# Second attention of a two-block network: values stationary, turned weights moving, softmax weights divided before they are turned

## The reference, cut to what matters

```python
def mla_attention(h, w_a, q_a_gain, kv_a_gain, w_qb, w_kvb, q_gain, k_gain, w_out, pos):
    ...
    scale = MLA_QK_DIM ** -0.5

    def block(blk, qb):
        sc = jnp.einsum('bqhd,bkhd->bhqk', qb, k).astype(jnp.float32) * scale
        p = causal_softmax(sc, blk, s)
        return jnp.einsum('bhqk,bkhd->bqhd', p.astype(v.dtype), v)

    o = query_block_map(block, q)
    return o.reshape(b, s, MLA_HEADS * MLA_V) @ w_out
```

## Time and profile before

| | |
|---|---|
| median of three executions | 1521.01 us |
| the executions | 1524.47, 1521.01, 1520.43 us |
| span of the profiled execution | 1517.0 us (its own time is not among those listed) |
| TensorE busy | 1321.8 us, 87% |
| VectorE busy | 664.2 us, 44% |
| ScalarE busy | 275.4 us, 18% |
| mean granted TensorE clock | 0.948 of 2.4 GHz |
| DMA | 512.58 MB, mean 338 GB/s |
| second attention, first turned weights to first `product` matmul | 666.89 to 701.51 us of the span |

### The profile page before, as it was taken

How to read it: one execution, slowest core, us unless ns; L and a number is a source line. 1 busy time by engine, 2 the same in 40 slices (tenths; PEclk the granted TensorE clock), 3 DMA queues, 4 the chain that set the end, 5 groups by cost and what they waited for, 6 DMA issues and landing times.

```text
span 1517.0 us, 25770 instructions
## 1 busy us (share of the span) xinstructions
PE 1321.8 (87%) x9790; PEld 825.2 (54%) x9790; DVE 664.2 (44%) x1596; ACT 275.4 (18%) x760; POOL 130.5 (9%) x199
## 2 busy tenths in 40 slices
PE   9999999767766779999999766767779999999997
PEld 4455565434433444566555433433344886899943
DVE  3874543211221222772543221221132634699976
ACT  2154111100100011362111100010011134222200
POOL 1312000000000000211000000000000133222100
PEclk9999999897988899999999988998899999999999
DMA  8978799999999999859799999999999980654400
GB/s 289 397 293 332 282 422 410 421 421 422 422 422 422 422 422 392 322 211 421 302 420 412 421 421 422 422 422 422 422 422 398 373 298 29 209 167 167 167 28 28
DMA packets 120379, 512.58 MB, mean 338 GB/s; under 512 B 12256, under 2 KB 46748, under 8 KB 69096
## 3 DMA queue, kind: packets, MB, share of 16 engines
q1 hardware_dynamic: 118576, 507.30, 83.9%
q0 software_dynamic: 1552, 4.06, 0.8%
q10 hardware_dynamic: 168, 0.09, 0.0%
HBM read 510.35 MB, written 1.07 MB: 337 GB/s over the span
## 4 chain that ended last, share of the span: by engine, by line
PE 36%; DMA 9%; SPq 8%; DVE 2%; issue 1%; POOL 0%; ACT 0%; POOLq 0%; DVEq 0%; ACTq 0%
DMA ring<-in_moe_w_up 9%; PE bank L2602 8%; SPq L1798 6%; PE bank L1365 5%; PE bank L2637 4%; PE bank L2219 3%; PE bank L439 2%; PE bank L451 2%; PE bank L1380 2%; PE bank L1351 2%; PE bank L1394 1%; SPq L1807 1%; PE bank L390 1%; PE bank L696 1%; PE bank L719 1%
## 5 line engine op out<-in xcount | busy, mean ns | idle before, releaser
L1365 PE MATMUL bank<-ring,hT 128*32 128x256 f32 (+1 forms) x2848 | 278.5, 456 | 137.9 <-DMA ring<-in_moe_w_up 74.3
L1365 PEld LDWEIGHTS bank<-ring,hT 128*32 128x32 f32 (+1 forms) x2848 | 146.8, 132 | 242.9 <-issue 183.4
L1645 DVE TENSOR_SCALAR pT<-pT 128x256 f32<-128x256 f32 x34 | 10.0, 294 | 441.8 <-ACT pT L1765 441.8
L1365 PE MATMUL bank<-BC,hT 128*32 128x256 f32 (+1 forms) x1120 | 141.3, 414 | 38.0 <-DMA ring<-in_moe_w_up 22.2
L1351 PEld LDWEIGHTS bank<-gtab,hn 128*128 128x128 f32 x1088 | 129.4, 192 | 15.4 <-issue 14.3
L1351 PE MATMUL bank<-gtab,hn 128*128 128x128 f32 x1088 | 132.6, 275 | 0.1
L1394 PE MATMUL bank<-hT,A 128*128 128x512 f32 x256 | 118.4, 605 | 0.0
L1380 PE MATMUL bank<-ring,gtab 128*32 128x512 f32 (+1 forms) x768 | 116.4, 595 | 0.9 <-ACT gtab L1759 0.9
L1365 PEld LDWEIGHTS bank<-BC,hT 128*32 128x32 f32 (+1 forms) x1120 | 73.1, 121 | 72.7 <-issue 54.0
L1765 ACT ACTIVATE pT<-bank 128x256 f32<-128x256 f32 x34 | 13.1, 384 | 484.4 <-PE bank L1365 484.4
L549 PE MATMUL bank<-ring,hT 128*128 128x512 f32 (+3 forms) x288 | 99.4, 505 | 0.3 <-DVE hT L313 0.2
(11 more groups left out here) (381 smaller groups left out, 1941.1 us busy)
## 6 DMA issues: line engine op xcount, KB each, us to landing
ring<-in_moe_w_gate SPq DMA_DIRECT2D x90, 1024.0 KB, 24.7
ring<-in_moe_w_up SPq DMA_DIRECT2D x88, 1024.0 KB, 25.5
ring<-in_moe_w_down SPq DMA_DIRECT2D x88, 1024.0 KB, 26.2
BC<-in_moe_w_gate SPq DMA_DIRECT2D x38, 1024.0 KB, 24.5
BC<-in_moe_w_up SPq DMA_DIRECT2D x32, 1024.0 KB, 25.0
BC<-in_moe_w_down SPq DMA_DIRECT2D x28, 1024.0 KB, 26.6
ring<-in_w_ada SPq DMA_DIRECT2D x24, 1024.0 KB, 14.8
ring<-in_w_up SPq DMA_DIRECT2D x22, 1024.0 KB, 5.8
```

The costliest lines, as they stand in the source:

```text
L1365: i = nc.tensor.matmul(GATE[q * cap:(q + 1) * cap, part * FF:(part + 1) * FF], xg[:, c, q * cap:(q + 1) * cap], u[:, c, :], start=(c == 0) ...
```

## The change

`o2` is made with `by_channel=True`. In the second attention:

- `weigh(i)` multiplies the item's weights in `SC` by `rden` right behind the reciprocal, on VectorE, and signals `mixed`; `turn(i)` waits for `mixed` and no longer for `exped`.
- `sum_v(i)` swaps its operands: the values are stationary, the turned weights move. The sum has channels on the partitions.
- `store(i)` is a plain copy to `hn`, by channel.
- `turn_heads` and `evac_heads` are left out for `o2`; `pieces` and `product` read `hn` head by head, each waiting for its own head's store. The 16 pieces stand two to an iteration from iteration 8 to 15.

```diff
+                self.by_channel, turns = by_channel, 0 if by_channel else TT
...
+            def channel(self, tt, c):
+
+                return hn[:, tt, c * P:(c + 1) * P] if self.by_channel else hT[:, c, tt * P:(tt + 1) * P]
...
             def heads_in(self, pe, tt, c):
+                if self.by_channel:
+                    self.heads_ready(pe, tt, c)
+                    return
...
             def tensor(self, pe, i, heads_ready):
 
+                if self.by_channel:
+                    self.heads_ready = heads_ready
+                    if i >= HEADS:
+                        self.pieces(pe, 2 * (i - HEADS), 2 * (i - HEADS) + 2)
+                    return
...
                 def turn(i):
                     tt, h, w = place(i)
-                    pe.wait_ge(*(mixed if mix else exped)(i + 1))
+                    pe.wait_ge(*(mixed if mix or by_channel else exped)(i + 1))
...
+                    if by_channel:
+                        for j in range(tt + 1):
+                            for m in range(outs):
+                                x = nc.tensor.matmul(out_bank[m * dv_w:(m + 1) * dv_w, 0:P], heads[h][1](j, m),
+                                                     turned_p[:, i % 3, m * w + j * P:m * w + (j + 1) * P],
+                                                     start=(j == 0), stop=(j == tt))
+                        x.then_inc(summed.sem, 1)
+                        return
...
             def heads_out(eng, tt, g):
-                if heads_ready:
+                if by_channel:
+                    eng.wait_ge(*stored(HEADS * tt + g + 1))
+                elif heads_ready:
...
-                    if i >= 3:
+                    if i >= 3 and not by_channel:
                         dve.wait_ge(*stored(i - 2))
                     dv.done(nc.vector.reciprocal(rden[:, i % 3, 0:maps], den[:, i % 3, 0:maps]))
+                    if by_channel:
+                        for m in range(maps):
+                            x = nc.vector.tensor_scalar(SC[:, i % 3, m, 0:w], SC[:, i % 3, m, 0:w],
+                                                        rden[:, i % 3, m:m + 1], None, ALU.mult)
+                        x.then_inc(mixed.sem, 1)
...
-                    if outs == 1:
+                    if by_channel:
+                        x = nc.vector.tensor_copy(dst, out_bank[:, 0:P])
+                    elif outs == 1:
...
-        o2 = OutStage(square_units(t["mla_w_out"][0], D, order="(c p)"), add_x)
+        o2 = OutStage(square_units(t["mla_w_out"][0], D, order="(c p)"), add_x, by_channel=True)
```

More of the change, by code:

```diff
@@ L392, in build, with __init__ @@
         class OutStage:
-            def __init__(self, blocks, add_to, heads_norm=None, gain=None):
+            def __init__(self, blocks, add_to, heads_norm=None, gain=None, by_channel=False):
                 self.blocks, self.add_to, self.heads_norm, self.gain = blocks, add_to, heads_norm, gain
+                self.by_channel, turns = by_channel, 0 if by_channel else TT
                 self.summed, self.added = shared("block_summed", 2), shared("block_added", 2 * TT)
-                self.turned = shared("turn_done", 4)
-                self.out_v, self.out_a = shared("turn_out_v", TT), shared("turn_out_a", TT)
+                self.turned = shared("turn_done", 2 * turns)
+                self.out_v, self.out_a = shared("turn_out_v", turns), shared("turn_out_a", turns)
+            def channel(self, tt, c):
+                return hn[:, tt, c * P:(c + 1) * P] if self.by_channel else hT[:, c, tt * P:(tt + 1) * P]
             def turn_bank(self, tt, g):
@@ L434, in pieces @@
                     self.heads_in(pe, 0, c)
-                    if n:
+                    if n and not self.by_channel:
                         self.heads_in(pe, 0, DC - 1)
@@ L438, in pieces @@
                     unit_here(pe, u)
-                    i = nc.tensor.matmul(bank[2 + n][:, :], hT[:, c, 0:P], view(slot(u))[:, c % 4, :], start=(c == 0),
+                    i = nc.tensor.matmul(bank[2 + n][:, :], self.channel(0, c), view(slot(u))[:, c % 4, :], start=(c == 0),
                                          stop=(c == DC - 1))
@@ L450, in product @@
                         self.heads_in(pe, 1, c)
-                        i = nc.tensor.matmul(bank[n][:, :], hT[:, c, P:S], view(slot(u))[:, c % 4, :], start=(c == 0),
+                        i = nc.tensor.matmul(bank[n][:, :], self.channel(1, c), view(slot(u))[:, c % 4, :], start=(c == 0),
                                              stop=(c == DC - 1))
@@ L499, in vector @@
                         self.heads_norm(dve, 0, 1)
-                if i == (HEADS + 2 if self.heads_norm else HEADS):
+                if i == (HEADS + 2 if self.heads_norm else HEADS) and not self.by_channel:
                     self.evac_heads(dve, 0, 1)
@@ L507, in vector_end @@
                     self.heads_norm(dve, 1, 1)
-                self.evac_heads(dve, 1, 1)
+                if not self.by_channel:
+                    self.evac_heads(dve, 1, 1)
         def project_stage(name, ready, lhs, blocks, evac, fold=None, sbanks=(0, 1, 2, 3), turn_next=None, parted=None,
@@ L663, in attention_stage @@
             outs = 1 if mix else maps
+            by_channel = out.by_channel
             scored, masked, maxed = (shared("head_scored", maps * items), shared("head_masked", maps * items),
                                      shared("head_maxed", TT * sink))
-            exped, mixed, turned = (shared("head_exped", items), shared("head_mixed", items if mix else 0),
+            exped, mixed, turned = (shared("head_exped", items), shared("head_mixed", items if mix or by_channel else 0),
                                     shared("head_turned", items))
```

## The result

The changed kernel takes **1524.03 us** (median of 20 runs, 1522.44 to 1525.69), the kernel before 1521.67 us on the same chips (20 runs, 1518.72 to 1524.47): a ratio of 1.0019, 95% interval 1.0013 to 1.0025. It is slower by 2.4 us. That is less than the 0.3% I had called the smallest that can be told, and is told all the same by 20 runs a side; it lies above my 1521.2 us, and just above the upper end of my range, 1524.0.

A forecast was written before the change was run, and what follows sets the result against it. The attention was taken as bound by a latency loop in tile 0 and TensorE in tile 1. Terms -1.75 + 1.15 + 0.45 + 0.3 = +0.15 us, added to the median, gave 1521.2 us; range 1518.8 to 1524.0.

The forecast's parts named there:

- the last sentence of the first part: Behind the second attention: a shift of its end reaches the kernel's end one for one, in either direction.
- if it begins where I say and the end still moves by over 2 us: Sign of error: `product` begins as forecast, yet the kernel's end moves; then the shift is not carried one for one.
- Rival E: The change does not do what it says, or the long weight stream sets in otherwise: chance 0.02, fast side.
- Rival B: Tile 0: fully serial loop, each turn in effect waiting for the previous item's store; about 1530 us, chance 0.03.
- C: TensorE's clock falls at the new wait at the attention's start: +3 to +5 us, 1525 us, chance 0.03.
- D: Loads released later by scores of items 11 and 15 are missed: some 3 us lost, 1524 us, chance 0.04.
- My other sign: Sign of error at the attention's end: `product` before 700.5 or after 703 us means a term is mis-sized.
- Removed turns: TensorE in the second attention: 16 head turns removed, all on the chain, -1.75 us.
- The first turn: Attention's start: the first turn waits for the first multiplication on VectorE, delaying the first `sum_v`; +1.15 us, bounds 1.1 and 1.3.
- Loop of tile 0 and edge: Items 1 to 7: two-item loop through store and multiplication, +0.45 us; wider masks and weights entering tile 1, +0.3 us.
- Tile 1 and the DMA of the attention: Items 8 to 15: multiplication hidden beside TensorE's work; later loads absorbed by 6 us of idle DMA; cost nothing.
- Sum of the attention: All terms of the second attention together: +0.15 us, bounds -0.65 and +1.35.

The follow-up runs named there:

- experiment 1: Changed kernel with 32 more TensorE instructions, long-satisfied waits ahead of the output projection's matmuls: 1521.17 us, ratio 0.9998 to the kernel before.
- experiment 3: Kernel before with 144 more satisfied TensorE waits in the projections ahead of the second attention: 1523.99 us, ratio 1.0015.
- experiment 8: Changed kernel with 16 more satisfied TensorE waits in the output projection: 1521.59 us in one run.
- experiment 2: Kernel before with 72 more satisfied TensorE waits in the projections ahead of the second attention: 1521.11 us, ratio 1.0000.
- experiment 7: Changed kernel with 32 more satisfied TensorE waits, but the multiplication by `rden` left out and the turn waiting for the exp: 1520.7 us in one run.

## Why the prediction was wrong

**The step that failed** is the last sentence of the first part: that "a shift of the attention's end is carried to the end of the kernel one for one". The attention got shorter by 0.4 us, and the kernel got slower by 2.4. I had treated the unchanged code behind the change as unaffected but for its start; yet the change moves every later TensorE instruction 32 places ahead, and that decides whether the mixture's loop is fetched once or again in each turn. I had named the sign of this ("if it begins where I say and the end still moves by over 2 us"), but not the mechanism, nor had any rival priced it. Rival E had "the long stream behind it sets in otherwise" at 0.02, and on the fast side. Rival B's 1530 us did not happen, nor C's fall of the clock at the attention's start (1.00 granted from 666 to 671 us), nor D's missed loads: from 700 to 830 us TensorE has one wait, 1.6 us for VectorE, as before. That D's 1524 us is near the measured time is chance. My other sign, `product` after 703 us, came up too (703.10 us), but by the place of the first mask and not by a term of the sum.

What the runs show in its place: -0.4 us from the attention and +2.9 us from instruction fetches, together +2.5 where +2.4 was measured. The -0.4 us stands in the traces; in the times alone experiment 1 is not told from the kernel before (0.9989 to 1.0007). That the fetches are the cause is shown by padding that switches them on without the change (experiment 3) and off with it (experiments 1 and 8), with the attention as long as it was each time. How the 2.9 us arise is shown in part. Between 894 and 1148 us the stream moves 107.13 - 106.45 = 0.68 MB fewer weights, and at 422 GB/s that is 1.6 us. The chain has the same matmuls (x16, ahead of the loop's wait for weights) at 803.63 us in experiment 1 and 803.40 in the changed kernel, which is still ahead there. The last expert's weights begin to be used at 1124.66 and 1127.82 us, 3.2 us apart, and from 1131 us to the end the distance is 2.8 us throughout. So the loss is made inside the loop, and nothing behind it adds to it. What is left of it beside the 1.6 us I can't divide between late buffers, the packets themselves and the lower clock behind each of the two waits. Why just these positions of the loop are fetched again is not shown either. The loop is 1656 instructions long (that many of TensorE's lie from one of its branches to the next in the trace), 6.5 pieces of 256. By my count of the stream, and if one piece is taken to be read ahead, it touches one piece more in the cases with fetches than in the others; that fits the kernels I counted (before, changed, and experiments 1, 2, 3 and 8), but no run measured the size of what the engine can hold.

**Removed turns, -1.75 us**: right in size. From the start of item 7's sum to `product` it is 25.35 us before and 23.66 after, 1.69 less; in experiment 7 it is 1.76 less.

**The first turn, +1.15 us**: right. The first turn came 1.52 us later relative to the first mask (forecast 1.44), the first `sum_v` 1.97 to 3.12 us behind the mask: +1.15. It got there with two errors that cancel: the multiplication takes 0.29 us and not 0.22, and behind the copy it is 0.07 us to the sum (671.21 to 671.28) and not 0.15. My interpolation between wide instructions missed that 128 columns take nearly as long as 256 (0.29 and 0.294 us), close to the `tensor_tensor` of the earlier trace rows, my upper bound. The estimate from the Trainium skill's figure (VectorE: DVE Perf Modes, the section on the TRN2 errata), 0.13 us for it, is further off still: 0.29 measured for 128 columns here, 0.354 for 256. That section of the Trainium skill says itself, beside its table, that the row gives too little for a single operation, which I left out.

**Loop of tile 0 and edge, +0.45 and +0.3 us**: mis-sized. Item 7's sum stands 9.99 us behind the first mask before and 11.28 after, so beyond the first turn's 1.15 us loop and edge cost 0.14 us, not 0.75. The loop cost nothing: from the sum of item 0 to that of item 4 it is 4.36 us before and 4.35 after. The edge has the rest, 3.66 and 3.81 us from item 4 to item 7. The sum for two items came out too long, 2.27 us where 0.94 + 1.21 = 2.15 was measured, by two gaps that I took from the earlier trace rows. "0.15 to TensorE" behind the copy is one: there the sum really waited for the store of the previous item (670.78 + 0.35 = 671.13, load at 671.24), and in the changed kernel the copy ends at 673.38 and the sum begins at 673.43. The 0.11 us from the end of a sum to its store is the other: it is 0.04 (671.74 to 671.78). The multiplication, 0.07 longer than forecast, takes back part of the two. The other side of the comparison was off too: I set 1.07 us an item against it, from one pair, where the first four steps of the kernel before take 1.09 on average and the last three, behind the wide scores of tile 1, 1.22.

**Tile 1 and the DMA of the attention, nothing**: right, `product` starts as soon as TensorE has worked off tile 1, and no load was missed.

**Sum of the attention**: +0.15 us forecast, -0.4 measured, inside its bounds of -0.65 and +1.35.

## What to carry to other kernels

Before an edit's sum is carried to the end of the kernel, look at the instruction queue on the page: an edit that only removes or adds instructions on an engine can move a long loop behind it so that it is fetched again in each turn. Here that fell into a DMA-bound stretch and cost 2.9 us, where the edit brought 0.4. The tell-tales are more packets on the instruction queue than before, and "issue" waits at the step from one turn to the next; a few idle waits as padding, ahead of the loop, test it in one run. And where two waits end near each other, take both releasers' ends away from the start before giving a gap to one of them: I gave one to the copy, and it was the store's.

## What the runs showed of the hardware

TensorE stood still for 9.14 and 9.26 us at the step of a loop while the DMA engines moved about 420 GB/s; the view of the queues counts the instruction packets and the weights against the same 16 engines (0.5% and 100.8%). Its clock fell during that. Windows of 2 us, after (PE busy, PEld, DVE, ACT, POOL, granted clock, DMA share, GB/s):

```profile
904.00:906.00 2.00, 0.00 (x0) 0.00 (x0) 0.39 (x2) 0.00 (x0) 0.00 (x0) 1.00 1.01 418
908.00:910.00 2.00, 0.00 (x0) 0.00 (x0) 0.00 (x0) 0.00 (x0) 0.00 (x0) 0.50 1.03 418
914.00:916.00 2.00, 2.00 (x24) 1.02 (x20) 0.00 (x0) 0.00 (x0) 0.00 (x0) 0.50 1.02 418
918.00:920.00 2.00, 2.00 (x44) 1.17 (x40) 0.00 (x0) 0.00 (x0) 0.00 (x0) 1.00 1.03 430
```

The granted clock goes to 0.50 (1.2 GHz) while the engine waits, stays there when it works again, and is back at 1.00 (2.4 GHz) by 918 us. Through the 1.54 us wait at the attention's start it stayed at 1.00.

Instructions ahead of a loop are not neutral, whichever way their number goes: 32 fewer cost 2.9 us, 72 more nothing, 144 more 2.9 us. A kernel's median can thus move by 0.2%, more than the interval of 11 or 20 runs, by an edit that does no work at all.
